# A bias-table store moved from GpSimd's queue to ScalarE's queue, in a hybrid attention step on one core

## The reference

```python
z = h @ w_in                       # 1056 tokens (1024 + 32) x 2848 columns
q_n, k_c, v_c, k_s, v_s, k_w, v_w, g, q_f, k_f, v_f, f = split(z)
kc, vc = compress(k_c), compress(v_c)            # blocks of 32 rows, stride 16, two small matmuls
lc = q_n @ kc * scale + t5_bias(t_pos - c_end)   # compressed, selected and window branches:
ls = q_n @ ks_selected * scale + t5_bias(dist)   # each adds the same table of 32 buckets x 8 heads
lw = q_n @ kw * scale + t5_bias(dist)
lf = q_f @ k_f * scale + decay                   # forgetting attention, no table
out = x + norm(concat(norm(o_n), norm(o_f)) @ w_o); out += norm(swiglu(norm(out)))
```

## Time and profile before

| | us |
|---|---|
| median of 3 runs | 1775.71 |
| lowest and highest | 1774.23, 1777.33 |
| the profiled execution | 1772.71 |
| its span | 1771.0 |
| TensorE busy in the span | 1695.1 (96%) |
| VectorE, ScalarE, GpSimd busy | 972.6, 722.3, 307.7 |

### The profile page before, as it was taken

How to read it: one execution, slowest core, us unless ns; L and a number is a source line. 1 busy time by engine, 2 the same in 40 slices (tenths; PEclk the granted TensorE clock), 3 DMA queues, 4 the chain that set the end, 5 groups by cost and what they waited for, 6 DMA issues and landing times.

```text
span 1771.0 us, 34560 instructions
## 1 busy us (share of the span) xinstructions
PE 1695.1 (96%) x13209; PEld 1522.6 (86%) x13209; DVE 972.6 (55%) x1889; ACT 722.3 (41%) x1481; POOL 307.7 (17%) x637
## 2 busy tenths in 40 slices
PE   7999999799897999999998999999999999999998
PEld 6999999676565878888886889999999999998886
DVE  4534342224355666767665568766666655465544
ACT  5201100222233778677776651233333333353342
POOL 3000005510503435353531000000000000000000
PEclk9999999899998999999999999999999999999999
DMA  5885756744999303030201233222222223964452
GB/s 143 237 190 155 239 172 119 233 118 172 310 337 275 94 11 99 1 109 1 97 2 57 93 110 117 73 85 73 73 76 94 73 73 113 407 192 147 142 152 75
DMA packets 144085, 236.28 MB, mean 133 GB/s; under 512 B 24297, under 2 KB 91288, under 8 KB 143858
## 3 DMA queue, kind: packets, MB, share of 16 engines
q1 hardware_dynamic: 110114, 159.36, 28.4%
q0 software_dynamic: 18480, 60.01, 11.1%
q10 hardware_dynamic: 15328, 14.72, 3.6%
HBM read 186.70 MB, written 51.49 MB: 134 GB/s over the span
## 4 chain that ended last, share of the span: by engine, by line
PE 83%; DVE 6%; DMA 4%; ACT 2%; issue 2%; SPq 2%; ACTq 1%; POOL 0%; DVEq 0%
PE psum L202 18%; PE psum L204 18%; PE psum L203 18%; PE psum L2135 5%; PE psum L2108 5%; PE psum L1195 4%; PE psum L2099 4%; PE psum L2100 2%; PE psum L1216 2%; DMA down_ring<-in_w_ffn_down 2%; SPq L377 1%; DMA fox_ring<-in_cache_fox_kv 1%; PE psum L1258 1%; PE psum L2143 1%; PE psum L557 1%
## 5 line engine op out<-in xcount | busy, mean ns | idle before, releaser
L202 PE MATMUL psum<-x_hi,w_hi 128*128 128x352 f32 x528 | 173.5, 329 | 0.0
L204 PE MATMUL psum<-x_hi,w_lo 128*128 128x352 f32 x528 | 170.5, 323 | 0.0
L203 PE MATMUL psum<-x_lo,w_hi 128*128 128x352 f32 x528 | 170.3, 323 | 0.0
L202 PE MATMUL psum<-hf_hi,op_hi 128*128 128x264 f32 x576 | 163.5, 284 | 0.6 <-DVE silu L3462 0.6
L204 PE MATMUL psum<-hf_hi,op_lo 128*128 128x264 f32 x576 | 163.5, 284 | 0.0
L203 PE MATMUL psum<-hf_lo,op_hi 128*128 128x264 f32 x576 | 163.3, 284 | 0.0
L2188 ACT ACTIVATE probs<-psum,neg_max 128x640 f32<-128x640 f32 (+7 forms) x192 | 139.9, 729 | 18.3 <-DVE neg_max L2346 9.0
L3472 DVE TENSOR_TENSOR down_lo<-down_ring,down_hi 128x1024 fp32r<-128x1024 f32 x66 | 80.8, 1225 | 113.1 <-ACT down_hi L3245 112.9
L2108 PE MATMUL psum<-ident,probs 128*128 128x128 f32 x848 | 129.1, 277 | 4.0 <-ACT probs L2188 2.5
L2198 ACT COPY probsT<-psum 128x512 f32<-128x512 f32 (+3 forms) x240 | 111.1, 485 | 52.9 <-PE psum L2108 51.5
L3245 ACT CAST down_hi<-down_ring 128x1024 fp32r<-128x1024 f32 x66 | 69.3, 1051 | 141.4 <-PE psum L204 104.5
(11 more groups left out here) (474 smaller groups left out, 4361.0 us busy)
## 6 DMA issues: line engine op xcount, KB each, us to landing
down_ring<-in_w_ffn_down SPq DMA_DIRECT2D x66, 512.0 KB, 3.8
fox_ring<-in_cache_fox_kv SPq DMA_DIRECT2D x128, 256.0 KB, 5.5
zT<-z_stage SPq DMA_DIRECT2D x22, 528.0 KB, 4.1
w_ring<-in_w_in POOLq DMA_DIRECT2D x22, 512.0 KB, 5.4
raw<-in_w_ffn_gate SPq DMA_DIRECT2D x9, 1024.0 KB, 7.9
raw<-in_w_ffn_up SPq DMA_DIRECT2D x9, 1024.0 KB, 5.4
h_dram<-stage POOLq DMA_DIRECT2D x8, 1056.0 KB, 6.0
nsa_page<-in_cache_nsa_kv POOLq DMA_DIRECT2D x64, 128.0 KB, 6.6
```

Of the source, the lines that this page charges most:

```text
L202: nc.tensor.matmul(dst, w_hi, x_hi, start=start, stop=False, skip_group_check=onto)
L203: nc.tensor.matmul(dst, w_hi, x_lo, start=False, stop=False, skip_group_check=onto)
L204: return nc.tensor.matmul(dst, w_lo, x_hi, start=False, stop=stop, skip_group_check=onto)
```

## The change

The store leaves GpSimd's stream, where it stood in `load_sampled` behind the last group's weight loads, and enters ScalarE's, behind the four `w1` loads and ahead of the wait for the gate stores. The condition it waits for, its source, its destination and its shape stay, as does GpSimd's wait for it at the end of the stage (`tab_stored`).

```diff
@@ -436,8 +436,6 @@
                     for br in range(3):
                         pool.dma_start(gates_dram[br].rearrange("s (h t) -> h s t", t=TS),
                                        gfT[GATE0 + br * H:GATE0 + (br + 1) * H, T:N].rearrange("h (s t) -> h s t", t=TS)).then_inc(gates_stored, 16)
-                    pool.wait_ge(head_dve, TAB_COPIED + 1)
-                    pool.dma_start(bias_tab, bias_vec[:, :].unsqueeze(1).to_broadcast([H, P, 384])).then_inc(tab_stored, 16)
                     pool.dma_start(w2k[:, DH:2 * DH], a["cmp_w2"][0, 0]).then_inc(w2_loaded, 16)
                     pool.dma_start(w2v[:, :], a["cmp_w2"][0, 1]).then_inc(w2_loaded, 16)
                     for kv in range(2):
@@ -621,6 +619,8 @@
             for kv in range(2):
                 for half in range(2):
                     act.dma_start(w1[half * DH:(half + 1) * DH, kv], a["cmp_w1"][0, kv].rearrange("(t d) n -> d t n", d=DH)).then_inc(w1_loaded, 16)
+            act.wait_ge(head_dve, TAB_COPIED + 1)
+            act.dma_start(bias_tab, bias_vec[:, :].unsqueeze(1).to_broadcast([H, P, 384])).then_inc(tab_stored, 16)
             act.wait_ge(gf_stored, 64)
             act.wait_ge(pages_loaded, 16)
```

## The result

The changed kernel takes 1779.34 us in the median of 20 runs (1775.41 to 1783.69), the kernel before 1774.22 us (20 runs on the same chip, 1772.07 to 1777.33). The ratio is 1.0027, 95% interval 1.0020 to 1.0035: slower by 5.1 us, small but outside 0.2%. The forecast was 1771.2 us, 4.5 us faster; the time lies just above its range too. The profiled execution has a span of 1779.9 us against 1771.0, 8.9 us more.

The account below looks back on a forecast made before the run. The table store was taken to hold SyncE's stores and idle TensorE at the projection's end. A gain of 8.5 us less 4 at the head gave -4.5: 1771.2 us against a 1775.7 median, range 1765.8 to 1779.

Parts of the forecast that it names:

- What bounds the kernel: Projection's end: the table store holds SyncE's stores, so TensorE idles 8.55 us before the transposes of chunks.
- the rival that blamed them: Projection's end: small loads, not the table, hold SyncE's queue in 284 to 306; 1777.7 us, chance 0.08.
- The tail's 8.5: Projection's end to the first product with w1: 8.5 us won, bounds 5 and 10, passing to the end.
- ScalarE's issue of the table costs nothing: New place behind w1: ScalarE is free at about 102 us, before it is wanted at 107.80; cost none.
- The store runs 107 to 140 to 144: Head: the table's data follow w1 from about 107 us and occupy the queue to 140 to 144.
- The 29 us: Head: estimate for the table store from two ports of 27.2 GB/s; it would end at 136, costs about zero.
- One for one: Table store's transfer: SyncE's store packets seem let through one for one with the table's, 52 each in 5 us.
- The first cost: Head, ScalarE: four key stores behind the table delay the copy of nat; TensorE waits about 1.3 us, 0 to 5.
- The second cost: Head, SyncE: slow page reads delay the first nat store; 2 to 6 us in all, first delay included, taken as 4.
- TensorE's clock falls in the projection: Rival, head: 7 to 10 us stall plus 2.5 to 5 of lowered clock; 1779.7 us, chance 0.17.
- The same stall in another place: Rival: all queues are held alike, the head loses what the tail wins, 8.5 us each; 1775.7 us, chance 0.08.
- two cases with 0.67 of the weight: The forecast itself (0.42, head cost 4 us) and the rival that the new place hides the store (0.25, 1767.2 us).

Follow-up runs that it names:

- e7b: Changed kernel with the table stored in two steps, a 12 KB row in DRAM first, then 128 copies from it, on ScalarE's queue: 1766.44 us, 0.9968.
- e8b: Kernel before, with the one-step table store kept on GpSimd's queue but moved to 114.2 us: 1791.74 us, 1.0096.
- e2: Changed kernel with tile 6's four key-part stores on GpSimd's queue instead of ScalarE's: 1778.13 us, 1.0029.
- e9: Changed kernel with tile 6's key stores on GpSimd's queue and SyncE's forget-log loads from the third round on one round later: 1778.40 us, 1.0022.
- e1: Table store issued by GpSimd in the sampled stage, at 362.6 us, out of the projection, against the kernel before: 1798.42 us, 1.0138.
- e4: Changed kernel with the table store on ScalarE's queue ahead of the four w1 loads instead of behind them: 1781.20 us, 1.0036.
- e5b: Kernel before, same place and queue, with the table stored in two steps through a DRAM row, copy outermost: 1769.73 us, 0.9976.
- e6b: Kernel before, same place and queue, two-step store through a DRAM row, with the head (8 rows) outermost: 1767.55 us, 0.9969.

## Why the prediction was wrong

**What bounds the kernel, right.** The table held the stores in 284 to 306. With the table elsewhere or in another form the stall is 1.0 us in all ten profiles, though the small loads stayed, which answers the rival that blamed them.

**The tail's 8.5, right in its own stretch, too large in all.** 9.5 us were won up to the first product with `w1`. The forecast stopped reading there. The sum then carried this gain to the end of the span, and 3.4 us of it were given back in the next 40 us as lowered clock. The term was worth about 6.

**ScalarE's issue of the table costs nothing, right.** It ended at 102.87 (forecast: about 102). e7b's store of only 12 KB in the same place took 9.72 us to issue against 9.92, so its length was that of the `w1` transfer ahead of it.

**The store runs 107 to 140 to 144, right.** It ran 106.7 to 142.1. The 29 us, estimated from the Trainium skill (page "SBUF — State Buffer", Door 1), are too short for this form: it took 35.1 to 42.0 us in the three kernels that show its landing, and 35.4 us from first packet to last here. "One for one" holds for SyncE's packets in the earlier trace rows but isn't a rule: in the same 5 us ScalarE's queue had 118 packets against the table's 52, and in 118 to 123 us of the changed kernel SyncE's had 85 against 140.

**The first cost, 1.3 us (0 to 5): the step that failed.** The words were "each of the next three needs a few freed places, about 1 us each". The next three took 3.91, 4.22 and 5.74, 13.9 in all; the first, which was to stand until 126, went out in 0.55. So the four stores took 14.5 us, the wait was 9.3 where 1.3 was put, and the margin of 1.5 us between copy and use, read rightly from the earlier trace rows, was far too small. The picture behind the step was wrong too: the stores were thought to be next in line in a queue half drained, and e8b shows 15.7 us with no table in that queue. The rows held the right picture: a `zT` store of another queue took 37.8 us beside the table, and a later issue on that queue stood 21.41. The forecast used these rows for SyncE and a kinder rule for ScalarE. In the sum, the head was put at 4 us and cost 12.9 in its first stretch, 10.2 of waits and 2.7 of lowered clock.

**The second cost, right in its place, too small, and not bound to its cause.** `nat` came free at 148.7, forecast 142 to 146, and e2 shows it alone as a wait of 9.9 us, forecast 2 to 6. The page reads were slow (1.95 us in the median, forecast 1.73), and SyncE's eight loads took 31.9 us and not 20. But e9, without them, has the wait all the same.

**The rivals.** "TensorE's clock falls in the projection" came true, given 0.17 and 1779.7 us: a stall of 9.3 us in one piece, 2.7 us of lowered clock behind it, 12.9 us with the other wait, inside its 10 to 15. Its trigger was to be a table that ends after 147; it ended at 142.1, and the stall came from the key stores. Nor does its limit of a stall of about 5 us hold: at 233 us of the changed kernel the clock fell behind a wait of 2.3 us, and at 336 behind one of 2.1. That the case came true is in part luck. "The same stall in another place" (0.08) was right in that every queue can be held: e1 and e4 show two more places, e8b another queue. It was wrong that the price is the same, since lowered clock comes on top at the head and the tail gives some back. The Trainium skill's rule named with it (page "DMA: Bandwidth & Descriptors", section "Issuing engines are not separate DMA queues") speaks for the right side of that: transfers of all issuers interleave on the same 16 engines, and e8b and the changed kernel, with other issuers of the table at about the same place, hold ScalarE's stores alike, 15.7 and 14.5 us. The chances were wrong in one way above all: two cases with 0.67 of the weight took the head's cost as 4 us or less, though the only stall behind this table in the trace cost 8.55. The range was too narrow as well: it leaves out the tail's own bounds of 5 to 10, and it stops at 1779 as the middle of the clock case, which is 1779.7, just beyond the measured time.

Open is what within the transfer is the limit: e5b and e6b show that the source in 8 partitions is what makes it long, not why. Open too is by what a store on a queue without the table is held at its issue. Open as well is the clock at 330 to 360 us, and in full the 1.3 us that arise ahead of the change.

## What to carry to other kernels

Before moving a long transfer, take its length, not its issue, as the time in which any other transfer on any queue may be held, and look for the shortest margin in that whole stretch, at issues as well as landings. If no stretch of that length is free, change the transfer: here a copy fanned out 128 times from 8 partitions took three to four times as long as the same bytes fanned out from DRAM, and after that the two places tried weren't clearly told apart. A stall won back isn't the gain until the next stretch has been read with its clock.

## What the runs showed of the hardware

- 1536 KB fanned out of 8 partitions took 35.1, 36.8 and 42.0 us on GpSimd's queue (e1, before, e8b; 48 GB/s in the quiet stretch of before) and, from first packet to last, 35.4 us on ScalarE's in the changed kernel (44 GB/s beside SyncE's loads); out of a row in DRAM 9.0 and 11.7 us, or 12.6 with 8 rows in the slowest dimension.
- Beside it, transfers of other queues were held: four stores on ScalarE's queue stood 12.3 to 15.7 us at their issue where they took 2.5, one of 16 KB on SyncE's 21.1 in e8b, a 512 KB store and the 16 KB one behind it took 32 us to land, and a weight load of GpSimd's 19.7 where it took 5.2.
- Which of two waits shows in the profile depends on which comes first: behind 9.3 us of one only 0.9 us of the other showed, and alone it was 9.9 us. The kernels with either issuing queue relieved, or both, had medians of 1778.1 to 1778.5 us and aren't told apart from the changed kernel's 1779.3.
